# Queries' norms as the exponential's scale, and the second attention's front in another order

## The reference

```python
q1 = rms_norm(q[..., 0, :], q_norm_g[i])          # per head: y * rsqrt(mean(y*y) + EPS) * g
k1 = rms_norm(k[..., 0, :], k_norm_g[i])          # the same for q2 and k2
att = softmax(mask(q1 @ k1.T / 8)) - lam * softmax(mask(q2 @ k2.T / 8))
...
cq, ckv, kr, gq, gk, gv = split(z)                # z = h @ w_in, h of the input and of the context
q = rmsnorm(cq, q_a_g) @ w_q_b                    # 8 latent heads of 64 + 32
gq, gk = rmsnorm(gq, q_norm_g), rmsnorm(gk, k_norm_g)
gq, gk, q_rope, k_rope = rope_2d(...)             # for the input's positions
softmax(q @ k.T / sqrt(d)) @ v
```

## Time and profile before

| | us |
|---|---|
| median of 3 runs | 3469.52 |
| lowest and highest | 3461.0 and 3470.22 |
| the profiled execution's own time | 3467.97 |
| its span in the trace | 3466.2 |
| PE busy in the span | 3294.7 |
| the stretch of the second front, 1791.28 to 1961.74 | 170.46 |
| PE busy in it | 141.92 |

### The profile page before, as it was taken

How to read it: one execution, slowest core, us unless ns; L and a number is a source line. 1 busy time by engine, 2 the same in 40 slices (tenths; PEclk the granted TensorE clock), 3 DMA queues, 4 the chain that set the end, 5 groups by cost and what they waited for, 6 DMA issues and landing times.

```text
span 3466.2 us, 36823 instructions
## 1 busy us (share of the span) xinstructions
PE 3294.7 (95%) x15132; PEld 2643.2 (76%) x15132; DVE 2064.2 (60%) x2663; ACT 1212.3 (35%) x1647; POOL 649.7 (19%) x495
## 2 busy tenths in 40 slices
PE   7999999999999999999988999989999988889998
PEld 5877777888787777888876776767777767768887
DVE  6655557664765555777556556555555578954443
ACT  3233432224432343322443243333333433332222
POOL 0000000000100002999710000002333024310000
PEclk9999999999999999999999899999999989999999
DMA  2222134552222224455321000022333231222222
GB/s 103 88 85 85 63 137 182 194 182 80 93 86 81 84 73 147 169 189 189 116 79 34 17 32 13 15 89 95 116 119 130 95 117 65 73 73 97 97 97 73
DMA packets 55624, 342.97 MB, mean 99 GB/s; under 512 B 5984, under 2 KB 7328, under 8 KB 18208
## 3 DMA queue, kind: packets, MB, share of 16 engines
q1 hardware_dynamic: 54080, 337.98, 27.4%
q10 hardware_dynamic: 1376, 2.62, 0.2%
HBM read 328.00 MB, written 12.58 MB: 98 GB/s over the span
## 4 chain that ended last, share of the span: by engine, by line
PE 69%; DVE 14%; POOL 10%; ACT 4%; issue 2%; DMA 0%; DVEq 0%; ACTq 0%; POOLq 0%
PE PS L262 68%; POOL FA L271 9%; DVE FA L279 3%; DVE wl L271 2%; PE PS L265 1%; DVE UL L271 1%; DVE SC L279 1%; ACT wh L268 1%; DVE SC L271 1%; ACT SC L268 1%; DVE SC L288 1%; DVE FA L288 1%; DVE PB L271 1%; ACT UH L268 1%; DVE FA L271 1%
## 5 line engine op out<-in xcount | busy, mean ns | idle before, releaser
L262 PE MATMUL PS<-UH,wh 128*128 128x512 f32 x2072 | 833.8, 402 | 42.2 <-DVE wl L271 21.4
L271 DVE TENSOR_TENSOR wl<-raw,wh 128x2048 fp32r<-128x2048 f32 (+2 forms) x255 | 562.3, 2205 | 443.1 <-ACT wh L268 443.0
L262 PE MATMUL PS<-UH,wl 128*128 128x512 f32 x2072 | 813.1, 392 | 0.0
L262 PE MATMUL PS<-UL,wh 128*128 128x512 f32 x2072 | 812.8, 392 | 0.0
L262 PE MATMUL PS<-RH,wh 128*128 128x512 f32 (+2 forms) x1688 | 671.3, 398 | 51.0 <-DVE RL L279 16.6
L262 PE MATMUL PS<-RL,wh 128*128 128x512 f32 (+2 forms) x1688 | 659.9, 391 | 0.0
L262 PE MATMUL PS<-RH,wl 128*128 128x512 f32 (+2 forms) x1688 | 659.3, 391 | 0.0
L268 ACT ACTIVATE wh<-raw 128x2048 fp32r<-128x2048 f32 (+2 forms) x255 | 454.5, 1783 | 320.1 <-PE PS L262 317.6
L262 PEld LDWEIGHTS PS<-UH,wh 128*128 128x128 f32 x2072 | 392.8, 190 | 160.3 <-issue 27.3
L262 PEld LDWEIGHTS PS<-UL,wh 128*128 128x128 f32 x2072 | 393.2, 190 | 84.3 <-issue 6.3
L262 PEld LDWEIGHTS PS<-UH,wl 128*128 128x128 f32 x2072 | 392.5, 189 | 83.6
(11 more groups left out here) (191 smaller groups left out, 3278.7 us busy)
## 6 DMA issues: line engine op xcount, KB each, us to landing
raw<-in_wall SPq DMA_DIRECT2D x224, 1024.0 KB, 4.8
FA<-in_wmod SPq DMA_DIRECT2D x48, 1024.0 KB, 4.9
raw<-in_wall SPq DMA_DIRECT2D x29, 512.0 KB, 3.5
kspec<-FA SPq DMA_DIRECT2D x8, 1024.0 KB, 7.1
FA<-kspec SPq DMA_DIRECT2D x8, 1024.0 KB, 4.8
PB<-in_window SPq DMA_DIRECT2D x16, 256.0 KB, 4.5
raw<-in_wall SPq DMA_DIRECT2D x8, 272.0 KB, 2.7
Hs<-in_xT ACTq DMA_DIRECT2D x4, 512.0 KB, 10.4
```

The lines of the kernel that those rows point to most:

```text
L262: return self.put(self.eng and self.eng.matmul(out, w, x, start=start, stop=stop, skip_group_check=True))
L271: return self.put(self.eng and self.eng.tensor_tensor(out, a, b, op))
```

## The change

It has five parts.

1. Layers: the four query tiles are no longer normalised. Their squares are summed by four matmuls of two columns each, with positions on the output's partitions, into one bank (`rq`). `query_roots` makes the inverse norms there as a 128 x 32 tile `RQ`, and its negative `NQ`. The exponential's scale and the factor of the maximum are columns of these. Queries' and keys' gains are multiplied into one. A score waits for the query tile's copy and no longer for its norm.
2. The second attention does the same with its four gq tiles and with the latent query cq. Of cq, ACT makes the high half and DVE the low half straight from PSUM, with the gain, and twelve matmuls of one column sum the squares.
3. `wh` and `wl` have three places instead of two. `raw` keeps two.
4. The context's halves are made in the second layer's gate stage, behind step 2, in the first four tiles of `UH` and `UL`; `norm_hi(6)`, which overwrites them, waits for the second gv group.
5. The front's products stand in another order, and gv's weights are loaded ahead of cq's.

The diff, cut to its core:

```diff
+PLACES = 3
...
+    load(("gv",), ("sum", ("cq", 2)), *[piece(A, 0, k * 128, 1, a, 128) for k in range(8) for a in (256, 1312)])
...
-    load(("gv",), ("sum", ("gv", 5)), *[piece(A, 0, k * 128, 1, a, 128) for k in range(8) for a in (256, 1312)])
...
     def C(k):
-        return pairf(2048 + NC * k, NC)
+        return UHf[:, NC * k:NC * k + NC], ULf[:, NC * k:NC * k + NC]
...
-        a = (place[i] % RAWS) * RAWN + o
+        a = (place[i] % PLACES) * RAWN + o
...
-              6: ("pr", 1, 7), 7: ("gv", 5), 8: ("up", 2, 3, 7), 9: ("iv", 3, 1, 3)}
...
+              6: ("gv", 1), 7: ("gv", 5), 8: ("up", 2, 3, 7), 9: ("iv", 3, 1, 3)}
...
-                p.wait_ge("qk_n", (l, h))
+                p.wait_ge("qk_x", (l, h))
...
+            p.wait_ge("hn_sq", (l, k))
+            if k < 4:
+                if k == 0:
+                    take(("rq", l), ("rq_m", l), held=True)
+                for i in range(4):
+                    p.matmul(ps(("rq", l), 2, o=8 * k + 2 * i), scr(("hn", l, k))[:, 128 * i:128 * i + 128], co["bd"][:, 0:128:64], True, True)
+                p.then_inc("sum", ("hn", l, k))
+                if k == 3:
+                    release(("rq", l))
+                return
...
+            def cq(m):
+                key, tag, o = ("cq", m), *((("gv",), 0) if m == 2 else (("cq",), 128 * m))
+                p.wait_ge("w_lo", tag)
+                take(key, ("cq_lo", m))
+                group(key, ps(key), [(pair(tag, 256 * k + o), U(k), u_made(6, k)) for k in range(8)])
+
+            def gq(k):
+                if k % 2 == 0:
+                    p.wait_ge("w_lo", ("gq", k // 2))
+                take(("gq", k), ("j_sq", ("q", k)))
+                group(("gq", k), ps(("gq", k)), [(pair(("gq", k // 2), 256 * i + 128 * (k % 2)), U(i), u_made(6, i)) for i in range(8)])
+
+            def gq_turn(k):
+                turned(("q", k), fat(GQ, k), 128, "rotG", [("a_in", ("gq", k)), ("ld_c2", 0)])
+
+            def latent_query_sums():
+                for m in range(3):
+                    p.wait_ge("j_sq", ("c", m))
+                for i in range(4):
+                    for m in range(3):
+                        p.matmul(ps(("rq",), 1, o=32 + i), query_square(("c", m))[:, 128 * i:128 * i + 128], ones[:, 0:1], m == 0, m == 2)
+                p.then_inc("sum", ("cs",))
+
+            def query_sums(k):
+                p.wait_ge("j_sq", ("q", k))
+                for i in range(4):
+                    p.matmul(ps(("rq",), 2, o=8 * k + 2 * i), query_square(("q", k))[:, 128 * i:128 * i + 128], co["bd"][:, 0:128:64], True, True)
+                p.then_inc("sum", ("rq", k))
...
+            both(kv, ("kv", 0), 0)
+            square_sums(6)
+            both(kv, ("kv", 1), 128)
+            both(gk, ("gk",), 0)
+            spread(6)
+            both(gk, ("kr",), 128)
+            p.wait_ge("w_lo", ("gv",))
+            for t in range(2):
+                gv(t)
+            latent_sum(0)
+            head_job(("k", 0))
+            jobs = [(kv, ("kv", 0, 1), 0), (kv, ("kv", 1, 1), 128), (gk, ("gk", 1), 0), (gk, ("kr", 1), 128)]
+            for tag, key, o in jobs:
+                take(key, ("a_in", key))
+            for k in range(8):
+                for e in u_made(6, k):
+                    p.wait_ge(*e)
+                for tag, key, o in jobs:
+                    three(ps(key), pair(tag, 256 * k + o), U(k), k == 0, k == 7)
+                    if k == 7:
+                        p.then_inc("sum", key)
+            gv(2)
+            gv(3)
+            latent_sum(1)
+            gv(4)
+            gv(5)
+            head_job(("k", 1))
+            turned(("kr",), fa(KM + 256, 512, 96), 96, "rotM", [("a_in", ("kr", 1)), ("ld_c2", 0)])
+            cq(2)
+            cq(0)
+            turned(("gk",), fa(KG + 256, 512), 128, "rotG", [("j_x", ("k", 1)), ("ld_c2", 0)])
+            cq(1)
+            take(("rq",), ("rq_ms", 0), held=True)
+            gq(0)
+            latent_query_sums()
+            gq(1)
+            gq_turn(0)
+            query_sums(0)
+            gq(2)
+            gq_turn(1)
+            query_sums(1)
+            gq(3)
+            gq_turn(2)
+            query_sums(2)
+            p.wait_ge("w_lo", ("vm",))
+            for t in range(3):
+                vm(t)
+            gq_turn(3)
+            query_sums(3)
+            release(("rq",))
+            for t in range(3, 6):
+                vm(t)
...
-                elif place[i] >= RAWS:
-                    a.wait_ge(*plan[ring[place[i] - RAWS]][5])
+                elif place[i] >= PLACES:
+                    a.wait_ge(*plan[ring[place[i] - PLACES]][5])
...
+                if k >= 6:
                     head_root(k - 2)
+                if k == 5:
+                    a.wait_ge("rq_m", l)
+                    a.activation(RQ[:, 0:32], RQ[:, 0:32], ACT.Sqrt).then_inc("rq_r", l)
...
+                    h, q = BLOCKS1[i]
+                    c = 8 * h + 2 * q + x
...
-                    a.activation(PB[:, b:b + nk], ps(("sc", l, i, x), nk), ACT.Exp, bias=st[:, 1:2], scale=0.125,
...
+                    a.activation(PB[:, b:b + nk], ps(("sc", l, i, x), nk), ACT.Exp, bias=st[:, 1:2], scale=RQ[:, c:c + 1],
...
+                if l == 1 and j == 2:
+                    context_hi()
...
-                a.wait_ge("sum", ("pg", 1, 7))
+                a.wait_ge("sum", ("dn", 1, 3, 7))
...
+            def query_roots():
+
+                r = RQ[:, 0:32]
+                v.wait_ge("sum", ("hn", l, 3))
+                v.tensor_scalar(r, ps(("rq", l), 32), 1.0 / 64, EPS, MUL, ADD).then_inc("rq_m", l)
+                v.tensor_tensor(ST[:, 6, 0:1], col("q_norm_g", l), col("k_norm_g", l), MUL)
+                v.wait_ge("rq_r", l)
+                v.reciprocal(r, r)
+                v.settle()
+                v.tensor_scalar(r, r, 0.125, None, MUL)
+                v.settle()
+                v.tensor_scalar(NQ[:, 0:32], r, -1.0, None, MUL)
...
-                v.stt(x, x, col("q_norm_g" if k < 4 else "k_norm_g", l), w, MUL, MUL).then_inc("qk_n", (l, k))
+                v.stt(x, x, ST[:, 6, 0:1], w, MUL, MUL).then_inc("qk_n", (l, k))
...
+            def cq_low(m):
+                h, lo = pairf(1536 + 512 * m, 512)
+                v.wait_ge("cq_hi", m)
+                v.wait_ge("j_sq", ("c", m))
+                v.stt(lo, ps(("cq", m)), col("a_q_a_g_2", 0, m), h.bitcast(F32), MUL, SUB).then_inc("cq_lo", m)
+
+            def query_roots():
+                v.wait_ge("sum", ("cs",))
+                v.wait_ge("sum", ("rq", 3))
+                v.tensor_scalar(RQ[:, 0:32], ps(("rq",), 32), 1.0 / 64, EPS, MUL, ADD)
+                v.tensor_scalar(RQ[:, 32:36], ps(("rq",), 4, o=32), 1.0 / 384, EPS, MUL, ADD).then_inc("rq_ms", 0)
+                v.wait_ge("rq_rt", 0)
+                v.reciprocal(RQ[:, :], RQ[:, :])
+                v.settle()
+                v.tensor_scalar(RQ[:, 0:32], RQ[:, 0:32], 0.125, None, MUL)
+                v.tensor_scalar(RQ[:, 32:36], RQ[:, 32:36], 1.0 / math.sqrt(96.0), None, MUL)
+                v.settle()
+                v.tensor_scalar(NQ, RQ[:, :], -1.0, None, MUL)
...
+            head_mean(0)
             latent(0)
-            w_lo(("gk",))
+            w_lo(("gv",))
+            head_norm(0)
             w_lo(("cq",))
             latent(1)
-            w_lo(("gq", 0))
-            head_mean(("k", 0))
-            head_mean(("k", 1))
-            head_norm(("k", 0))
-            head_norm(("k", 1))
+            head_mean(1)
+            head_norm(1)
             rope(("kr",), fa(KM + 256, 512, 96), 96, "M")
             v.settle()
             v.tensor_copy(FA[64:96, KM + 768:KM + 1536], FA[64:96, KM:KM + 768]).then_inc("gk2", "kr")
-            head_mean(("q", 0))
-            head_norm(("q", 0))
-            w_lo(("gq", 1))
+            w_lo(("gq", 0))
+            cq_low(2)
+            cq_low(0)
             rope(("gk",), fa(KG + 256, 512), 128, "G")
             v.settle()
             v.tensor_copy(FA[0:64, KG + 768:KG + 1536], FA[64:128, KG:KG + 768]).then_inc("gk2", 0)
             v.tensor_copy(FA[64:128, KG + 768:KG + 1536], FA[0:64, KG:KG + 768]).then_inc("gk2", 1)
-            head_mean(("q", 1))
-            head_norm(("q", 1))
-            gq_rope(0)
-            head_mean(("q", 2))
-            head_norm(("q", 2))
-            w_lo(("gv",))
-            head_mean(("q", 3))
-            head_norm(("q", 3))
-            gq_rope(1)
-            gq_rope(2)
+            cq_low(1)
+            w_lo(("gq", 1))
+            for k in range(3):
+                gq_rope(k)
+            w_lo(("vm",))
             gq_rope(3)
-            w_lo(("vm",))
-            r = fa(VM, 512)
-            job_mean(("c",), r, 512, 384)
-            v.wait_ge("j_rt", ("c",))
-            v.reciprocal(r, r)
-            v.settle()
-
-            def latent_low(k):
-                h, lo = pairf(1536 + 512 * k, 512)
-                v.wait_ge("cq_hi", k)
```

(15 more changed lines are left out.)

229 lines of the change are left out of this document (93 added, 136 removed).

## The result

The changed kernel took 3417.48 us (median of 4 runs, 3414.28 to 3419.85), the kernel before in the same measurement 3465.26 (4 runs). The ratio is 0.9859, with an interval from 0.9843 to 0.9876: 1.4% faster, 47.8 us, where I had forecast 38.6 and 3431. The value lies half a microsecond under my range. Of the 13.5 us between 3431 and 3417.5, 9.2 are gain beyond my sum, and 4.3 are the base: I had counted from a median of 3469.5 for the kernel before, and in this measurement it was 3465.3.

The account below looks back on a forecast made before the run. PE was taken as the bound (busy 3294.7 of 3466.2 us), with 42.5 us in the second attention's front that are no work. Terms summed to -38.6, giving 3431 us; forecast's own range 3426 to 3437, full range 3418 to 3449.

Parts of the forecast that it names:

- -26.3 + 2.1: Second attention's front: 26.3 of 28.5 us of PE waits go; new waits of 0.6 before U and 1.5 at gk's turn.
- -14.0 + 1.2: Front: all 14.0 us lost to half clock return with the waits gone; a fall after the one-column sums costs 1.2.
- +0.1: Second attention's queries on PE: seven float32 matmuls go (-6.0), two-column and one-column sums come (+6.1), together +0.1 us.
- my walk through the new order: Front: group by group timing from 1791.28; the stretch to the first block score should last 130 us instead of 170.
- -2.5 + 0.3: Layers: waits of 1.5 and 1.0 us before the eighth head sum go; PE's eight head sums cost 0.3 us more.
- +0.5: Block loop: the exponential's second memory operand, 88 ns each, is hidden save at the loop's ends: +0.5 us (0 to 11).
- A: Rival, front: half clock stays because gv groups and sums are light work wherever they stand; 3441 us, chance 0.16.
- B: Rival, front: the waits move, turns and vm's first groups find operands 3 us late, 15 come back; 3446 us, chance 0.08.
- C: Rival, block loop: ACT's longer exponentials are on the path, 11 us more; 3442 us, chance 0.04.
- D: Rival: more than the sum, with no fall, no new waits and the third place helping elsewhere; 3423 us, chance 0.10.
- E: Rival: slower, every light piece lets the clock fall and heavy products start at half; 3491 us, chance 0.03.
- F: Rival, front: U's chain stays late, waits behind the norms and half clock stay; 3461 us, chance 0.03.

Follow-up runs that it names:

- both kernels that split further ahead: Changed kernel with weight tiles split two ahead, outside the front everywhere: 3422.10 us; only in the second half's MLPs and at Hyena's first tile: 3409.79 us.
- the one with part 4 undone: Changed kernel with the context's halves made right ahead of the front again, not in the gate stage: 3432.47 us, ratio to before 0.9910.
- the load put back: Changed kernel plus idle DVE work (one reciprocal, five cheap operations) before each rope of gq, which each turn waits for: 3438.49 us, ratio to before 0.9925.
- The kernel without interleaving: Changed kernel with the four products of kv, gk and kr made one after another, not k by k: 3426.42 us, ratio to before 0.9883.
- the second and third trace of before: The kernel before, unchanged, profiled two more times: spans of 3459.3 and 3454.7 us, against 3466.2 in its first trace.
- the constants: Changed kernel with constants for the exponentials' scale column and the maxima's factor column, softmax flat: 3424.60 us, ratio to before 0.9882.
- the one shown: Trace of the kernel before with part 3 alone, three places for split weights: ratio 1.0001; its front took 175.3 us.

## Why the prediction was right or wrong

The mechanism was right and the sum too small. The front gave -42.7, where its terms made -36.9; the layers gave -1.3, where I had -2.2; the block loop cost 2.5, where I had 0.5. That makes some -41.5 for the -38.6 of the sum. The rest of the first measurement's 47.8 is falls and a start that differ from one execution to the next.

**Waits: right.** I had -26.3 + 2.1 = -24.2 and got 28.5 less 3.0, -25.5. The wait before U is 0.5 for my 0.6, that of the turn of gk 0.9 for my 1.5, and the two kept ones are 1.5 for 2.2.

**Half clock: nearly right.** I had -14.0 + 1.2; it was -14.4 and 0. The +1.2 for a fall after the twelve one-column sums was a fair size for the wrong kind of thing: it is 0 or 1.7. The three traces of the changed kernel have none. Of all ten traces with the new order four have one: both kernels that split further ahead, whose fronts are 1.6 us longer, the one with part 4 undone, and the one with the load put back. That the clock comes back when the waits go is shown by the load put back (waits of 6.5, half clock of 8.0 at them). One reading was wrong: the window 1908.80, which I gave as gv matmuls at full clock without a wait before them, holds a wait of 0.64 us before its turn. There a wait of 0.64 us left the clock up.

**PE's own work in the front: the step that failed.** I took the time between waits as work, whose only change was +0.1 by counting matmuls. PE's busy time at full clock fell from 127.5 (141.92 less 14.4) to 124.89, by 2.6. The exchange of matmuls was priced nearly right. A turn with the query sums behind it takes 2.23 us up to the third matmul that follows, 1.78 more than two steps of 0.227, where I had 0.86 + 0.90; the 12 one-column sums take 2.7 by the same measure for my 2.5:

```profile
1882.64 1.02 PE L263 MATMUL PS<-FA,CO 128*128 128x512 f32 x2
1883.50 0.95 PE L263 MATMUL PS<-CO,FA 128*128 128x2 f32 x8
1884.31 0.49 PE L263 MATMUL PS<-UH,wh 128*128 128x512 f32 x1
...
1884.87 0.40 PE L263 MATMUL PS<-UH,wl 128*128 128x512 f32 x1
```

What went is, as I read it, the restart: 16 waits became 4, and each has a price beyond its booked length that I had put at nothing. To make up 2.6 it would have to be 0.2 for each of the 12. The kernel without interleaving has six waits more and 1.9 us more of busy time, 0.3 each; the second and third trace of before have four waits fewer than the first and 1.0 us less of busy time at full clock, some 0.25 each; the load put back has four more waits and 0.5 more, 0.1 each; and with part 4 undone, one wait more, nothing is to be seen. So 0.2 lies in the middle of what the runs show, but no run gives it for these very waits.

**The walk and the sum.** By my walk through the new order the front would last 130 us instead of 170, 40 less, and I summed 36.9 for the same stretch. The two were not set against each other; the walk was within 2.1 us.

**Layers.** Of -2.5 + 0.3 the waits did go; a fall of the clock behind the sums took 1.7 back in the first layer, and 3.4 in three of ten traces. I had asked for such a fall in the front and not here, where the sums also stand behind a wait (0.68 us).

**The exponential's operand: sized too small.** I had +0.5 because ACT is busy for 77 of 200 us. Its share of busy time was the wrong thing to look at: PE's waits for ACT in the block loop grew by 2.5 us, and 2.2 of them went with the constants.

**Outside the front: the range was too narrow.** On the mean the falls that come and go there cost both kernels the same to 2 us, so the 0 that I took was right for them. But I took the scatter from three runs; one kernel's falls outside the front cost 32.7 to 47.6 us in three traces, and its medians were 3417.5 and 3427.5. The second of these lies in my range, and so does the mean, 3421.0: that the first set fell just outside is luck.

Rivals: A was not seen in the new order. B, late turns, came only with the load put back. C did not come with its 11 us; 2.3 did. D's third place gave 0 as long as the program did not use it, and some 9 us once the second half did. E and F did not come.

## What to carry to other kernels

Where one engine is the bound, price a wait by three numbers: its length, a restart (0.1 to 0.3 us here), and the half clock behind it, which in this front came to half the length of the waits (14.4 for 28.5). Price what you put on a helping engine in a tight loop by the waits for it, and not by its busy share. Put the work that needs nothing (here gv over the context) where the wait was, and let the next product take each operand as it is made, so that one piece feeds several outputs. Compare two kernels by a stage's length in the traces before trusting a median: the front was the same to 0.1 us in three traces where two medians of the same kernel differed by 10.

## What the hardware showed that I had not expected

- One kernel, executed again, has other falls of the clock. After the shift products the 6.20 us were at 0.50 and 0.72 in traces of before, and at 0.72 and 1.00 in traces of the changed kernel, with the same instructions; a fall there cost 1.7 us or 3.4.
- A fall during which PE waits for DVE anyway costs nothing. In the second and third trace of before the clock also fell behind the first wait for UL (3.0 us lost), PE waited for 26.4 us instead of 28.5, and the front was as long as in the first to 0.1 us.
- Once down, the clock stayed down for as long as the gv groups lasted: 8.5 us lost in four of the five traces with the old order, 17 in the one shown.
